# Two softmax attentions with a pair's values in one bank, and the feed-forward entries in another order

## The reference

```python
for layer in range(2):
    hn = rms_norm(x, norm_mix_pre[layer])
    if layer == 0:
        mix = sparse_attn_conv_mixer(hn, ...)   # 8 heads of 64; top-128 keys; beside it a short convolution
    else:
        mix = mla_mixer(hn, ...)                # 16 heads: q, k of 64 + 32 (rotary), v of 64
    x = x + rms_norm(mix, norm_mix_post[layer])
    hn = rms_norm(x, norm_ffn_pre[layer])
    x = x + rms_norm(square(relu(hn @ w1)) @ w2, norm_ffn_post[layer])
# in both mixers, per head:
p = softmax(where(allowed, q @ k.T * scale, -inf))   # 512 x 512, causal
o = p @ v                                            # 512 x 64
```

## Time and profile before

| | |
|---|---|
| three runs, us | 1906.57, 1898.72, 1902.23 (median 1902.23) |
| the profiled execution, us | 1901.33, its span 1899.6 |
| PE busy | 1831.5 us, 96% |
| DVE, ACT, POOL busy | 883.4, 744.7, 625.3 us |
| mean granted TensorE clock | 0.99 of full speed |

### The profile page before, as it was taken

How to read it: one execution, slowest core, us unless ns; L and a number is a source line. 1 busy time by engine, 2 the same in 40 slices (tenths; PEclk the granted TensorE clock), 3 DMA queues, 4 the chain that set the end, 5 groups by cost and what they waited for, 6 DMA issues and landing times.

```text
span 1899.6 us, 22688 instructions
## 1 busy us (share of the span) xinstructions
PE 1831.5 (96%) x9025; PEld 1483.0 (78%) x9025; DVE 883.4 (47%) x1337; ACT 744.7 (39%) x1236; POOL 625.3 (33%) x215
## 2 busy tenths in 40 slices
PE   7999999999998899999999999998999999999998
PEld 4787777778787667878888888877788788888886
DVE  6411467556746359852533333353366253233334
ACT  3324555545234343353522223245545252222232
POOL 1433121232243323402434433433300243344342
PEclk9999999999999999999999999999999999999999
DMA  7533222221131322202222232222200222222322
GB/s 284 199 110 107 67 69 55 56 68 66 45 133 51 100 67 89 100 23 78 89 89 88 89 110 89 89 90 85 89 1 1 78 87 80 100 88 93 106 89 78
DMA packets 83379, 165.11 MB, mean 87 GB/s; under 512 B 5977, under 2 KB 8158, under 8 KB 83294
## 3 DMA queue, kind: packets, MB, share of 16 engines
q1 hardware_dynamic: 83294, 163.95, 26.2%
HBM read 157.64 MB, written 2.10 MB: 84 GB/s over the span
## 4 chain that ended last, share of the span: by engine, by line
PE 72%; issue 16%; DVE 5%; POOL 4%; ACT 3%; DMA 1%; SPq 0%; POOLq 0%; DVEq 0%; ACTq 0%
PE PDT L631 11%; PE PDT L633 11%; PE PDT L632 11%; PE PDT L642 7%; PE PDT L644 7%; PE PDT L643 7%; POOL wlo L1822 4%; PE PM L1223 3%; PE PM L1193 1%; PE PDT L1193 1%; PE PM L1172 1%; PE PDT L771 1%; PE PDT L777 1%; PE PDT L772 1%; PE PM L679 1%
## 5 line engine op out<-in xcount | busy, mean ns | idle before, releaser
L1822 POOL TENSOR_TENSOR wlo<-wraw,whi 128x2048 fp32r<-128x2048 f32 (+4 forms) x166 | 612.9, 3702 | 1240.0 <-ACT whi L1326 1200.7
L1326 ACT ACTIVATE whi<-wraw 128x2048 fp32r<-128x2048 f32 (+2 forms) x133 | 247.9, 1864 | 543.9 <-PE PDT L633 319.2
L642 PE MATMUL PDT<-hhi,whi 128*128 128x512 f32 x800 | 316.0, 395 | 5.8 <-ACT mh_r L1445 5.0
L644 PE MATMUL PDT<-hhi,wlo 128*128 128x512 f32 x800 | 312.3, 390 | 0.0
L643 PE MATMUL PDT<-hlo,whi 128*128 128x512 f32 x800 | 312.3, 390 | 0.0
L631 PE MATMUL PDT<-whi,hhi 128*128 128x512 f32 (+1 forms) x612 | 244.4, 399 | 4.3 <-DVE hlo L1927 3.6
L632 PE MATMUL PDT<-wlo,hhi 128*128 128x512 f32 (+1 forms) x612 | 237.7, 388 | 0.0
L633 PE MATMUL PDT<-whi,hlo 128*128 128x512 f32 (+1 forms) x612 | 237.5, 388 | 0.0
L631 PE MATMUL PDT<-whi,mh_hi 128*128 128x512 f32 x512 | 202.5, 396 | 0.0
L633 PE MATMUL PDT<-whi,mh_lo 128*128 128x512 f32 x512 | 202.5, 396 | 0.0
L632 PE MATMUL PDT<-wlo,mh_hi 128*128 128x512 f32 x512 | 202.4, 395 | 0.0
(11 more groups left out here) (343 smaller groups left out, 2477.2 us busy)
## 6 DMA issues: line engine op xcount, KB each, us to landing
wraw<-in_mlp_w SPq DMA_DIRECT2D x64, 1024.0 KB, 5.2
wraw<-in_w_in SPq DMA_DIRECT2D x26, 1024.0 KB, 5.1
wraw<-in_even_w_in SPq DMA_DIRECT2D x16, 1024.0 KB, 5.3
w_ada<-in_w_ada SPq DMA_DIRECT2D x12, 1024.0 KB, 13.7
wraw<-in_w_out SPq DMA_DIRECT2D x8, 1024.0 KB, 5.1
swapped<-qk_sb SPq DMA_DIRECT2D x16, 256.0 KB, 6.7
wraw<-in_even_w_out SPq DMA_DIRECT2D x4, 1024.0 KB, 5.6
wraw<-in_odd_w_o SPq DMA_DIRECT2D x4, 1024.0 KB, 5.1
```

The lines of the kernel that those rows point to most:

```text
L642: mm(bank, sth, hi[:, k0 + k, :], start=start and k == 0, stop=False)
L644: last = mm(bank, stl, hi[:, k0 + k, :], start=False, stop=stop and k == 3)
L1326: nc.scalar.activation(whi[base % 2][:, 0:n], wraw[base % 2][:, 0:n], ACT.Copy).then_inc(S("w_hi"), 1)
L1822: part = g.tensor_tensor(wlo[base % 2][:, cols], wraw[base % 2][:, cols], fl(whi[base % 2][:, cols]), ALU.subtract)
```

## The change

It has four parts.

1. Values by pairs. For two heads, prt now holds four buffers, v is the stationary operand (128x64) and the turned probabilities move, so that the result has the features on the partitions: head 2p in partitions 0 to 63 of PM bank 3, head 2p+1 in 64 to 127. The turned blocks are laid out by key block for this (KEY_FIRST). Key blocks 1, 3, 2 of a pair stand in one iteration of the loop, block 0 in the next.
2. The denominators. They are per query, and the queries now lie along the free dimension. DVE inverts den (invert), POOL widens it to 64 columns per head (widen), PE transposes it (turn_den, four transposes per pair into PDT bank 3), ACT copies it to lat (turned_den), DVE multiplies PM bank 3 with it (over_den), ACT and DVE take the high and the low part right into hhi and hlo (lat_high, lat_low). The transposes and splits after the loops are gone.
3. Order on ACT in the loop: the copy of the turned probabilities stands between the second and the third exponential, where it stood behind the fourth.
4. Feed-forward entries: C1 stands before M2 on DVE, and the rounding of the fourth weight unit stands behind the second high part on ACT, where it stood before the first. A gain row (row_b) is loaded later, since its place is now used by the loops.

```diff
-    FFN_ORDER = ["M0", "X0", "M1", "X1", "B0", "B1", "C0", "M2", "C1", "M3", "X2", "X3", "B2", "B3", "C2", "C3"]
+    FFN_ORDER = ["M0", "X0", "M1", "X1", "B0", "B1", "C0", "C1", "M2", "M3", "X2", "X3", "B2", "B3", "C2", "C3"]
...
-        sp.wait_ge(S("tr_read"), TR["lat"][0])
+        sp.wait_ge(S("att_out"), (A_H + C_H) // 2)
+        load(row_b[:, :], norm_mix_post_2[1].partition_broadcast(P), "row_b_loaded")
         load(row_c[:, :], norm_ffn_pre_2[1].partition_broadcast(P), "row_pre")
...
+        def turn_den(pair, wide):
+
+            pe.wait_ge(S("den_wide"), 2 * pair + 2)
+            pe.wait_ge(S("tr_read"), den_group(pair))
             for t in range(TT):
...
+                last = nc.tensor.transpose(PDT[:, 3, t * P:t * P + P], wide[pair % 2][:, t, :], ident[:, :])
+            last.then_inc(S("tr_done"), 1)
+
+        def pair_values(pair, first, keys, pt, v):
+
+            if keys[0]:
+                probs_taken(2 * pair + 2)
+                if pair:
+                    pe.wait_ge(S("att_out"), pair)
+            for s in keys:
+                a, w = KEY_FIRST[s], SEQ - s * P
+                for half in range(2):
+                    c0 = (2 * (pair - first) + half) * HD
+                    last = mm(PM[HD * half:HD * half + HD, 3, s * P:SEQ], v[:, s, c0:c0 + HD],
+                              pt[(2 * pair + half) % 4][:, a:a + w], start=s == 1, stop=s == 0, skip_group_check=True)
+            if keys[0] == 0:
+                last.then_inc(S("att_pv"), 1)
...
-            if h >= 2:
-                values(n - 2, prt3, lambda j: v3[:, j, (h - 2) * HD:(h - 1) * HD])
-        pe.wait_ge(S("att_out"), A_H + C_H)
-        transposes("lat", 8, lambda t, k: v3[:, t, k * P:k * P + P])
-        transposed("lat", 8)
+            if h >= 3 and h % 2:
+                pair_values((n - 3) // 2, A_H // 2, (1, 3, 2), prt3, v3)
+                turn_den((n - 3) // 2, den_wide3)
+            elif h >= 4:
+                pair_values((n - 4) // 2, A_H // 2, (0,), prt3, v3)
+        pe.wait_ge(S("tr_read"), TR["ffn1"][0])
+        pe.wait_ge(S("attn_low"), KT + (A_H + C_H) // 2)
         two_units("wo3", 0, 0, 0, 2, False)
...
                 relu(1)
-                if peeled and first == 0:
-                    hi(0, u0 + 3, 0)
                 part(0)
                 relu(2)
                 part(1)
+                if peeled and first == 0:
+                    hi(0, u0 + 3, 0)
                 relu(3)
...
             if h < C_H:
-                exps(A_H + h, pr3, mx3, den3)
-            if h:
-                turned(A_H + h - 1, prt3)
+                exps(n, pr3, mx3, den3, ((0, 3), (1, 2)))
+            if 1 <= h <= C_H:
+                turned(n - 1, prt3)
+            if h < C_H:
+                exps(n, pr3, mx3, den3, ((2, 0), (3, 1)))
+            if h >= 5 and h % 2:
+                lat_high((n - 5) // 2, (h - 5) // 2)
+            if h >= 3 and h % 2 and h < C_H + 3:
+                turned_den((n - 3) // 2)
...
+        def widen(n, d, wide):
+
+            pair, c0 = n // 2, HD * (n % 2)
+            pool.wait_ge(S("den_ready"), n + 1)
+            if pair >= 2:
+                pool.wait_ge(S("tr_done"), den_group(pair - 2) + 1)
+            g.tensor_copy(wide[pair % 2][:, :, c0:c0 + HD], d[:, n % 4, :].unsqueeze(2).to_broadcast([P, TT, HD]))\
+                .then_inc(S("den_wide"), 1)
...
+            if pair is not None:
+                over_den(pair)
             if h < C_H:
-                row_least(A_H + h, mx3, lambda t: causal[:, (3 - t) * P:SEQ])
+                row_least(n, mx3, lambda t: causal[:, (3 - t) * P:SEQ])
             if 1 <= h <= C_H:
-                turned(A_H + h - 1, prt3)
+                turned(n - 1, prt3)
             if h + 2 < C_H:
                 turned_k(h + 2)
-            if h >= 2:
-                emit(A_H + h - 2, den3, v3[:, :, (h - 2) * HD:(h - 1) * HD])
+            if 1 <= h <= C_H:
+                invert(n - 1, den3)
+            if pair is not None:
+                lat_low(pair, pair - A_H // 2)
```

More of the change, by code:

```diff
@@ L242, in build_program @@
     pr = [arena("pr0", [P, 1280], 8), arena("pr1", [P, 1280], 13)]
-    prt = [arena("prt0", [P, 1280], 18), arena("prt1", [P, 1280], 23)]
+    prt = [arena(f"prt{s}", [P, 1280], kb) for s, kb in enumerate((18, 23, 60.5, 69.5))]
+    lat = [at(f"lat{s}", [P, SEQ], offset=place["junk"] + 2 * KB * s) for s in range(2)]
+    den_wide = [arena(f"den_wide{s}", [P, TT, 2 * HD], 28 + 2 * s) for s in range(2)]
     mx = arena("mx", [P, 4, TT], 77.625)
@@ L396, in gate_at, with head_group, den_group @@
         return za[:, (k + 4) % KT, :]
+    def head_group(h, m):
+        return TR["heads"][0] + 2 * h + m + max(0, (h - 4) // 2)
+    def den_group(pair):
+        if pair < A_H // 2:
+            return TR["den2"][0] + pair
+        pair -= A_H // 2
+        return TR["heads"][0] + 2 * min(C_H, 2 * pair + 6) + pair
     def idx_pair(t, tile):
@@ L1235, in _ @@
                 turn_probs(h - 1, pr)
-            if h >= 2:
-                values(h - 2, prt, lambda j: v2[:, j, (h - 2) * HD:(h - 1) * HD])
+            if h >= 3 and h % 2:
+                pair_values((h - 3) // 2, 0, (1, 3, 2), prt, v2)
+                turn_den((h - 3) // 2, den_wide)
+            elif h >= 4:
+                pair_values((h - 4) // 2, 0, (0,), prt, v2)
         pe.wait_ge(S("conv2_done"), 4)
         wo2 = pieces("wo2", 1)
-        piece(*wo2[0])
-        pe.wait_ge(S("att_out"), A_H)
-        for n in range(3):
-            transposes("attn", n + 1 + n // 2, lambda t, k: v2[:, t, k * P:k * P + P], n)
-            piece(*wo2[n + 1])
-        transposed("attn", 4)
+        pe.wait_ge(S("tr_read"), TR["den2"][0] + A_H // 2)
+        for p in wo2[:4]:
+            piece(*p)
+        pe.wait_ge(S("attn_low"), KT + A_H // 2)
         for p in wo2[4:]:
@@ L1290, in _ @@
             turn_qk(h, 1)
-        for h in range(C_H + 2):
+        for h in range(C_H + 3):
             n = A_H + h
@@ L1716, in exps @@
             if n >= 4:
-                act.wait_ge(S("att_out"), n - 3)
-            for q, t in enumerate((3, 2, 0, 1)):
+                act.wait_ge(S("den_wide"), n - 3)
+            for q, t in order:
                 b, c0 = QB_AT[t]
@@ L1791, in _ @@
         turned_q(1)
-        for h in range(C_H + 1):
+        act.wait_ge(S("w_used"), PH["wo3"][0])
+        for h in range(C_H + 4):
+            n = A_H + h
             if h + 2 < C_H:
@@ L1890, in _ @@
         pairs("gates", 3)
+        def widen(n, d, wide):
+            pair, c0 = n // 2, HD * (n % 2)
+            pool.wait_ge(S("den_ready"), n + 1)
+            if pair >= 2:
+                pool.wait_ge(S("tr_done"), den_group(pair - 2) + 1)
+            g.tensor_copy(wide[pair % 2][:, :, c0:c0 + HD], d[:, n % 4, :].unsqueeze(2).to_broadcast([P, TT, HD]))\
+                .then_inc(S("den_wide"), 1)
+        for n in range(A_H):
+            widen(n, den, den_wide)
         units("wo2", "mlp0")
@@ L1907, in _ @@
         units("uq", "wo3")
+        for n in range(A_H, A_H + C_H):
+            widen(n, den3, den_wide3)
         units("wo3", "mlp1")
```

127 lines of the change are left out of this document (69 added, 58 removed).

## The result

The changed kernel takes 1874.26 us (median of four runs, 1872.19 to 1877.5) against 1902.87 us for the kernel before (four runs): ratio 0.9852, interval 0.9827 to 0.9877. The prediction said 1873, with a range of 1864 to 1888, and the change makes the kernel faster. The profiled execution took 1874.76 us in a span of 1873.0, which is 26.6 us less than the span before. The changed program was measured a second time, beside another kernel (experiment 10): 1876.38 us, ratio 0.986 (0.9838 to 0.9881), with a profiled span of 1876.5. So a term of 2 or 3 us can't be read from one time; it has to be read at its place in the trace, and the clock at that place belongs to the reading.

The account below looks back on a forecast made before the run. PE was taken to bound both attention loops. Gains of 14.7 (second attention), 5.0 (first), 7.2 (feed-forward) and 1.7 (clock) sum to 28.6; 1901.3 - 28.6 = 1873 us, range 1864 to 1888.

Parts of the forecast that it names:

- Values in pairs, the pace (7.6): Second attention, heads 3 to 14: a pair takes 11.45 us, the loop 67.9 instead of 75.5, gain 7.6 us.
- The toll of the form: Value products of a pair: entering and leaving the paired form adds 0.2 us to the even part, 0.1 to the odd.
- The second loop's start (1.9) and end (5.2): Second attention: earlier copy and no values in iteration 2 gain 1.9 us; last logits to output layer 13.6, gain 5.2.
- First attention (5.0): First attention: shorter iterations, partly held by DVE, and no transposes in the output layer gain 5.0 us, between 2 and 7.
- Feed-forward (7.2): Both feed-forward entries: PE's waits of 1.10 and 2.49 us go at each, gain 7.2 us together.
- rival 3: Feed-forward wait comes back elsewhere (fourth bank or next weights): 5 us back, 1878 to 1880 us; chance 0.04.
- Clock (1.7): Behind the second attention's end: half clock after the long wait loses 1.7 us; 1.7 gained, between 0 and 3.4.
- 1: Value products: the two heads' products don't overlap, a pair's values cost 4.6 us, total 1894 us; chance 0.07.
- 2: Attention loops keep their old pace, bound by ACT's and DVE's orders with mutual waits: 1886 us; chance 0.13.
- rival 4: Attention loops: PE falls to half clock and stays there, up to 128 us lost, 1970 us or more; chance 0.04.

Follow-up runs that it names:

- experiment 10: The changed kernel itself, unedited, measured once more beside another kernel: 1876.38 us, ratio 0.986 to the kernel before.
- Experiment 5: Changed kernel with the value products of both heads of a pair written to the same output rows, 0 to 63: 1898.13 us, ratio 0.9958 to the kernel before.
- experiment 4: Changed kernel with ACT's copy of the turned probabilities put back behind the fourth exponential: 1884.89 us, ratio 0.988 to the kernel before.
- Experiment 2: Changed kernel with only ACT's rounding of the fourth weight unit put back ahead of the first high part: 1881.27 us, one run.
- experiment 1: Kernel before with only the two feed-forward edits (C1 before M2 on DVE, ACT's rounding behind the first high parts): 1895.76 us, ratio 0.995.

## Why the prediction held, and the one term that did not

- **Values in pairs, the pace (7.6).** Right in mechanism and size: 11.49 us a pair for 11.45. Experiment 5 shows the cause, experiment 4 that ACT's new order is needed for it. The toll of the form was put at 0.2 and 0.1 inside the products; it shows as 0.2 in the logits and 0.15 in the denominators behind them, and in the same size in experiment 5, where nothing runs in pairs (2.36 and 0.59). The Trainium skill's rule (TensorEngine Tiling (Array Packing), Tiling Modes) that a change of mode drains the engine agrees with these two rows; as priced it was right.
- **The second loop's start (1.9) and end (5.2).** The end gave 4.9. The stretch from first to last logits gave 7.3, not 9.5, because the first logits took 4.13 us at half clock where they took 2.16 before: without these 2.0 it is 9.3. The change is not needed for the half clock there: the kernel with the feed-forward edits alone, whose attentions are those of before, has it as well (first logits 4.27 us). The profile of before was the only one of ten without it.
- **First attention (5.0).** 5.0 after taking off the 1.10 of the feed-forward entry: 3.1 in the loop and 1.85 where the sixteen transposes were. DVE holds one of the later heads, by 0.8 us, and the last values by 0.9.
- **Feed-forward (7.2).** The waits went, and rival 3 did not come: DVE's stall moved to a square that nobody waits for. Experiment 2 brings the wait back with one instruction. That DVE's whole instruction is held while POOL's runs (the Trainium skill, SBUF — State Buffer, SBUF: two separate sides) agrees with the 4.65 and the 4.72.
- **Clock (1.7): the step that failed.** "After the long wait at 1476 to 1482.75 PE runs at a granted 0.76", and then "The new wait there is 2.3 us. I take 1.7 off". The first part is a misreading. The chain of waits shows DVE's low parts in that stretch, but PE was busy 4.42 of its 6.75 us with the transposes:

```profile
1476.43 1.97 PE L679 MATMUL PM<-ident,v 128*128 128x128 f32 x16 [0.59 <-DVE v L2385]
1478.56 2.45 PE L679 MATMUL PM<-ident,v 128*128 128x128 f32 x16 [0.16 <-DVE hlo L1927]
1482.75 0.50 PE L631 MATMUL PDT<-whi,hhi 128*128 128x512 f32 x1 [1.74 <-DVE hlo L1927]
```

  Its longest wait there was 1.74 us. The new one is 2.23 and so longer, not shorter, and nothing in the rows gave a reason to expect the half clock gone. In the profile after, the output layer still runs at half clock (products 0.43 apart from 1463.47 on; the row from 1461 to 1471 above has 0.83), as in four more of the eight profiles that keep the wait. Nor was the half clock of before fixed to that place: in experiment 1, with the same end of the attention, it lies ahead of the 1.74 us wait (last values 4.10 us), and the layer behind it has 0.23 from its start. So no run shows a credit of 1.7 for a wait that only changes its length.
- **What filled its place was luck.** The half clock of before behind the second 2.49 us wait (granted 0.85 and 0.94 over 1560 to 1576) is gone, and the last stretch gives 4.5 us where the wait alone gives 2.5. The prediction had left that out of its sum and allowed it only as its upper end. It does not come with every such wait either: of the four in the profiles of before and of experiment 2 two have it behind them. This 2.0 us and the missing 1.7 nearly cancel; the 2.0 us lost at the second loop's start is then about what the 26.6 us of gain in the spans lack against the 28.6 predicted.
- **Rivals.** 1 is refuted by the 1.45 and 1.01 us and by experiment 5, 2 by the pace, 3 by PE's missing waits, 4 by the granted clock: 0.97 from 1363 to 1450 us with the start included. The mechanism that rival 4 feared does exist in small: about 2 us at most places, up to 4.3 in the first attention of the changed kernel's second profile, never a whole loop. Whether the two places in the loops' beginnings would be hit in each execution, the profiles leave open.

## What to carry to other kernels

Products with few output columns per head are worth turning round only where two of them can run in different column halves: paired they took 56% of the old time, unpaired 105%. An instruction that waits long should not stand ahead of short ones others need; moving one rounding behind three short ones was worth a 2.49 us wait, twice. A PE wait of 2.2 to 2.5 us can cost up to 1.7 us more by half clock behind it, in some executions and not in others: count it over several profiles before a term is made of it. And a stretch in which the chain of waits names another engine is not a stretch in which PE waits: read PE's own rows for that.

## Not expected of the hardware

- A 2.23 us wait of PE is followed by about 3 us of half clock in five of eight profiles, and one of 2.49 us by the same in two of four. No row that was read tells the one kind from the other.
- Two executions of one program differ by 3.5 us in span, most of it through a half-clock stretch (the first attention takes 45.22 and 49.52 us, granted 1.00 and 0.76). What calls it up in one execution and not in the other stays open.
- Pairs whose heads stand one after the other still take less than two single heads (2.14 against 2.73 us for blocks 1, 3 and 2). Likely the last product of one half runs beside the first of the other; no row shows it by itself.
